# First mixer: rotary key columns first with their weights stationary, latents normed singly, query products between transposes

## The reference, cut to what matters

```python
def mla_mixer(h, cos, sin, w_in, g_qa, w_qb, g_kva, w_kvb, g_q, g_k, w_o):
    z = h @ w_in                                  # 2048 -> 512 + 512 + 64
    c_q, c_kv, k_rope = jnp.split(z, [512, 1024], axis=-1)
    q  = (rms_norm(c_q,  g_qa)  @ w_qb ).reshape(b, s, 16, 192)
    kv = (rms_norm(c_kv, g_kva) @ w_kvb).reshape(b, s, 16, 256)
    k_nope, v = jnp.split(kv, [128], axis=-1)
    k = concatenate([k_nope, k_rope for every head])
    q, k = rms_norm(q, g_q), rms_norm(k, g_k)     # over 192 columns of a head
    q, k = (each with its last 64 columns rotated by cos, sin)
    o = blocked_attention(q, k, v, 1 / sqrt(192), chunk_causal=True)
    return o.reshape(b, s, 2048) @ w_o
```

## Time and profile before

| | us |
|---|---|
| median of 3 runs | 3583.55 (3583.06 to 3585.41) |
| the profiled execution | 3579.43 |
| its span | 3577.5 |
| granted TensorE clock, mean | 0.917 of 2.4 GHz |

### The profile page before, as it was taken

How to read it: one execution, slowest core, us unless ns; L and a number is a source line. 1 busy time by engine, 2 the same in 40 slices (tenths; PEclk the granted TensorE clock), 3 DMA queues, 4 the chain that set the end, 5 groups by cost and what they waited for, 6 DMA issues and landing times.

```text
span 3577.5 us, 26686 instructions
## 1 busy us (share of the span) xinstructions
PE 2869.6 (80%) x7322; PEld 1347.5 (38%) x7322; DVE 2037.9 (57%) x3580; ACT 946.3 (26%) x2345; POOL 1422.9 (40%) x1065
## 2 busy tenths in 40 slices
PE   7888967777777888888878788998987877777776
PEld 6445743333332333333333333443433322222222
DVE  2334156666767554555554665455555466777765
ACT  3334322222222222323221222232322122222221
POOL 4002645565665322222432432322333255555553
PEclk8877989998998999999999899999999998888888
DMA  4212599999999999999999999999999999999998
GB/s 145 83 62 81 194 384 416 416 414 417 416 417 422 418 417 417 417 417 418 416 419 417 413 417 417 417 417 417 416 400 419 417 408 418 418 417 420 415 417 357
DMA packets 246468, 1345.34 MB, mean 376 GB/s; under 512 B 27200, under 2 KB 48192, under 8 KB 113984
## 3 DMA queue, kind: packets, MB, share of 16 engines
q0 software_dynamic: 147456, 1073.81, 72.5%
q1 hardware_dynamic: 98880, 269.99, 19.8%
HBM read 1341.62 MB, written 2.10 MB: 376 GB/s over the span
## 4 chain that ended last, share of the span: by engine, by line
DMA 64%; PE 20%; issue 11%; DVE 3%; POOL 1%; ACT 1%; SPq 1%; DVEq 0%; POOLq 0%; ACTq 0%
DMA room<-in_peer_v_dram,index 64%; PE psum L982 12%; PE psum L1033 3%; PE psum L745 1%; PE psum L746 1%; PE psum L747 1%; POOL room L673 1%; DVE room L1962 0%; DVE resid L1973 0%; POOL room L683 0%; DMA room<-in_peer_u_dram,index 0%; SPq L544 0%; POOL w_low L657 0%; SPq L514 0%; PE psum L948 0%
## 5 line engine op out<-in xcount | busy, mean ns | idle before, releaser
L982 PE MATMUL psum<-room,diag 128*128 128x512 f32 x3072 | 1636.2, 675 | 628.1 <-DMA room<-in_peer_v_dram,index 581.6
L1962 DVE CUSTOM_DVE_ANT_0 room<-room,normed 128x2048 f32<-128x2048 f32 x512 | 1172.9, 2291 | 664.4 <-DMA room<-in_peer_u_dram,index 660.0
L982 PEld LDWEIGHTS psum<-room,diag 128*128 128x128 f32 x3072 | 607.2, 210 | 1595.4 <-issue 1257.2
L683 POOL DMA_INDIRECT room<-in_peer_v_dram,index x512 | 748.5, 1462 | 1070.2 <-PE psum L982 1039.9
L673 POOL DMA_INDIRECT room<-in_peer_u_dram,index x512 | 558.3, 1090 | 757.9 <-DVE dots L1962 529.6
L1033 PE MATMUL psum<-wbuf,normedT 128*128 128x512 f32 x1536 | 695.1, 595 | 0.0
L1392 ACT ACTIVATE acts<-dots 128x1 f32<-128x1 f32 x512 | 103.6, 202 | 1832.2 <-DVE dots L1962 1831.8
L1973 DVE SCALAR_TENSOR_TENSOR resid<-room,acts,resid 128x512 f32<-128x512 f32 x512 | 384.4, 751 | 290.9 <-DMA room<-in_peer_v_dram,index 289.1
L1033 PEld LDWEIGHTS psum<-wbuf,normedT 128*128 128x128 f32 x1536 | 285.3, 191 | 330.7 <-issue 327.6
L657 POOL TENSOR_TENSOR w_low<-wbuf,w_high 128x2048 fp32r<-128x2048 f32 (+1 forms) x28 | 113.9, 4076 | 305.1 <-ACT w_high L1247 305.1
L1401 ACT ACTIVATE diag<-ident,acts 128x128 f32<-128x128 f32 x512 | 205.5, 401 | 48.3 <-ACT acts L1396 1.5
(11 more groups left out here) (197 smaller groups left out, 1742.8 us busy)
## 6 DMA issues: line engine op xcount, KB each, us to landing
wbuf<-in_fox_w_in_dram SPq DMA_DIRECT2D x128, 1024.0 KB
wbuf<-in_fox_w_o_dram SPq DMA_DIRECT2D x32, 1024.0 KB
wbuf<-in_peer_w_q_dram SPq DMA_DIRECT2D x32, 1024.0 KB
wbuf<-in_mla_w_o_dram SPq DMA_DIRECT2D x16, 1024.0 KB, 5.2
wbuf<-in_peer_w_q_dram SPq DMA_DIRECT2D x32, 512.0 KB, 8.9
wbuf<-in_mla_w_in_dram SPq DMA_DIRECT2D x8, 1024.0 KB, 8.2
wbuf<-in_mla_w_kvb_dram SPq DMA_DIRECT2D x32, 256.0 KB, 3.5
room<-in_peer_u_dram,index POOLq DMA_INDIRECT x512
```

The lines of the kernel that those rows point to most:

```text
L683: pool.indirect_dma_start(v_ring[:, r, :], None, v_table, bass.IndirectOffsetOnAxis(index[:, number % 2, s:s + 1], 0)).then_inc(v_full[r], 16)
L982: mm = pe.matmul(psum[:, q, :], diag[:, r, :], v_ring[:, r, q * TILE:(q + 1) * TILE], start=at == 0, stop=at == WINDOW - 1, skip_group_che ...
L1962: V.tensor_tensor_reduce(u_ring[:, r, :], u_ring[:, r, :], normed[:, b, :], 1.0, 0.0, ALU.mult, ALU.add, dots[:, r:r + 1]).then_inc(dot_do ...
```

## The change

1. The 64 rotary columns of `w_in` get a buffer of their own in `room`. SP loads them in one DMA ahead of the first tile; ACT and POOL split them behind the first quarter of that tile. PE multiplies them right behind the transposes of the normed tokens, with the weights (64 columns) stationary and the 256 tokens moving: 48 matmuls in place of 96. The result lies transposed and is turned back by two small transposes behind those of the sub-keys. DVE does the rotary keys first.
2. Each latent is normed by itself. The query latent's transposes stand inside the second tile, behind its sixth and seventh eighth.
3. The four query pieces of group g+1 stand one ahead of each of the four transposes of group g; the four key/value pieces behind the first four attention steps. ACT copies the query products ahead of the attention. Each weight buffer is given back by itself: that of keys/values behind T(q,1), that of queries behind the first attention step, the last one behind the last group's transposes.

The diff, cut to its core:

```diff
             w_in = rows_view(mla_w_in[0])
-            widths = (Q_RANK, KV_RANK, ROPE)
-            for t in range(3):
-                c0 = sum(widths[:t])
-                load_quarters(S_IN + t, 0, w_in, slice(c0, c0 + widths[t]), widths[t], free=t == 0)
+            sp.dma_start(rope_w, w_in[:, :, Q_RANK + KV_RANK:Q_RANK + KV_RANK + ROPE]).then_inc(rope_loaded, 16)
+            for t in range(2):
+                load_quarters(S_IN + t, 0, w_in, slice(t * Q_RANK, (t + 1) * Q_RANK), free=t == 0)
                 if t == 0:
                     small_operands()
...
-            for t, width in enumerate((Q_RANK, KV_RANK, ROPE)):
-                low_parts([S_IN + t], width)
+            pool.wait_ge(unit_high, 1)
+            pool.tensor_tensor(quarter(w_low, 0), values(0), quarter(w_high, 0), ALU.subtract).then_inc(unit_low, 1)
+            pool.wait_ge(rope_split, 1)
+            pool.tensor_tensor(rope_low[:, :, :], rope_w, rope_high[:, :, :], ALU.subtract).then_inc(rope_split2, 1)
+            low_parts([S_IN], 1)
+            low_parts([S_IN + 1])
...
+            def rope_keys():
+                pe.wait_ge(rope_split2, 1)
+                for k in range(KC):
+                    pe.matmul(dst, rope_high[:, k, :], x_high[:, k, :], start=k == 0, stop=False)
+                    pe.matmul(dst, rope_low[:, k, :], x_high[:, k, :], start=False, stop=False)
+                    last = pe.matmul(dst, rope_high[:, k, :], other[:, k, :], start=False, stop=k == KC - 1)
+                last.then_inc(rope_full, 1)
+            def rope_transposes():
+                pe.wait_ge(rope_out, 1)
+                for b in range(NB):
+                    last = transpose(psum[:, 6, T + b * ROPE:T + (b + 1) * ROPE],
+                                     raw_v[0:ROPE, 0, T + b * P:T + (b + 1) * P], ROPE)
+                last.then_inc(rope_turned, 1)
...
+                def turned(t, b):
+                    pe.wait_ge(lat_norm, 2 * t + b + 1)
+                    if t:
+                        pe.wait_ge(lat_done, b + 1)
+                    for c in range(RC):
+                        last = transpose(sbank(b)[:, c * P:(c + 1) * P], (qn, kn)[t][:, b, c * P:(c + 1) * P])
+                    last.then_inc(lat_full, 1)
+                split_gemm(S_IN, 0, Q_RANK, x_high, other)
+                split_gemm(S_IN + 1, 0, KV_RANK, x_high, other,
+                           steps=[lambda: None] * 5 + [lambda: turned(0, 0), lambda: turned(0, 1)])
+                for b in range(NB):
+                    turned(1, b)
+            def qk_transposes(at, g, kind, ahead):
                 src = (qn, kn)[kind]
                 for b in range(NB):
+                    if ahead:
+                        ahead.pop(0)()
                     at.qk_norm.done(pe, g, 2 * kind + b)
                     if kind == 0:
...
-                        if b == NB - 1 and t:
-                            for t2 in range(2):
-                                (wh, wn), (gh, gn) = mla.w(g, t2), mla.g(g, t2)
-                                pe.wait_ge(g_full[gh], 2 * gn + 2)
-                                pe.sem_inc(w_used[wh], 1)
...
+            def release(g, t):
+                (wh, wn), (gh, gn) = mla.w(g, t), mla.g(g, t)
+                pe.wait_ge(g_full[gh], 2 * gn + 2)
+                pe.sem_inc(w_used[wh], 1)
...
+                pe.wait_ge(lat_done, 2)
+                run(mla_products(0, 0))
                 pe.wait_ge(lat_done, 4)
-                run(mla_products(0))
+                kv = mla_products(0, 1)
+                run(kv[0:2])
+                release(0, 0)
+                run(kv[2:4])
                 with pe.Fori(0, mla.groups - 1) as g:
-                    for kind in range(2):
-                        qk_transposes(mla, g, kind)
-                    steps, pieces = attention(mla, g), mla_products(g + 1)
-                    for i in range(max(len(steps), len(pieces))):
-                        run(steps[i:i + 1])
-                        run(pieces[i:i + 1])
+                    ahead = mla_products(g + 1, 0)
+                    qk_transposes(mla, g, 0, ahead)
+                    release(g, 1)
+                    qk_transposes(mla, g, 1, ahead)
+                    steps, kv = attention(mla, g), mla_products(g + 1, 1)
+                    for i, step in enumerate(steps):
+                        step()
+                        if i == 0:
+                            release(g + 1, 0)
+                        run(kv[i:i + 1])
                 for kind in range(2):
-                    qk_transposes(mla, mla.groups - 1, kind)
+                    qk_transposes(mla, mla.groups - 1, kind, [])
+                release(mla.groups - 1, 1)
                 run(attention(mla, mla.groups - 1))
...
             norm_transposes(0)
+            rope_keys()
             sub_keys()
+            rope_transposes()
...
                     copy_transposed(p, b)
+                    if p == 0 and b == 0:
+                        act.wait_ge(rope_loaded, 16)
+                        nc.scalar.activation(rope_high[:, :, :], rope_w, ACT.Copy).then_inc(rope_split, 1)
...
+                high_parts(S_IN + 1, qs=range(3))
+                copied(0, raw_q)
+                high_parts(S_IN + 1, qs=range(3, 4))
+                root(0)
+                turned(0)
+                copied(1, raw_k)
+                root(1)
+                turned(1)
...
                 with act.Fori(0, mla.groups - 1) as g:
                     both_transposed(g)
-                    attention(mla, g, lambda step: step == COPY_Q_AT and copy_q(g + 1))
+                    copy_q(g + 1)
+                    attention(mla, g)
                     copy_kv(g + 1)
...
+            act.wait_ge(rope_full, 1)
+            nc.scalar.activation(raw_v[0:ROPE, 0, T:2 * T], psum[0:ROPE, 6, 0:T], ACT.Copy).then_inc(rope_out, 1)
             act.wait_ge(keys_full, 1)
             nc.scalar.activation(keysT[:, :, :], psum[:, 7, :].rearrange("p (m n) -> p m n", m=4),
                                  ACT.Copy).then_inc(keys_done, 1)
+            act.wait_ge(rope_turned, 1)
+            nc.scalar.activation(raw_v[:, :, 0:ROPE], psum[:, 6, T:T + 2 * ROPE].rearrange("p (b r) -> p b r", b=NB),
+                                 ACT.Copy).then_inc(rope_done, 1)
...
             def latent():
+                dve.wait_ge(rope_done, 1)
                 for b in range(NB):
...
                 chain.settle()
+                for t, (raw, g) in enumerate(((raw_q, g_qa), (raw_k, g_kva))):
+                    for b in range(NB):
+                        dve.wait_ge(evac[(G_IN + t) % 2], 2 * ((G_IN + t) // 2) + b + 3)
+                        last = sum_squares(raw[:, b, :], (qn, kn)[t][:, b, :], l_sum[:, 2 * t + b:2 * t + b + 1])
+                    last.then_inc(lat_ss, 1)
+                    dve.wait_ge(lat_root, t + 1)
+                    step(V.reciprocal(l_inv[:, 2 * t:2 * t + 2], l_root[:, 2 * t:2 * t + 2]))
+                    chain.settle()
+                    for b in range(NB):
+                        V.scalar_tensor_tensor(out=(qn, kn)[t][:, b, :], in0=raw[:, b, :],
+                                               scalar=l_inv[:, 2 * t + b:2 * t + b + 1], in1=g[:, :],
+                                               op0=ALU.mult, op1=ALU.mult).then_inc(lat_norm, 1)
```

More of the change, by code:

```diff
@@ L340, in hybrid_encoder @@
         unit_full = [sem(f"unit_full{q}") for q in range(4)]
+        rope_loaded, rope_split, rope_split2, rope_full, rope_out, rope_turned, rope_done = (
+            sem(n) for n in ("rope_loaded", "rope_split", "rope_split2", "rope_full", "rope_out", "rope_turned",
+                             "rope_done"))
         unit_high, unit_low, unit_used = sem("unit_high"), sem("unit_low"), sem("unit_used")
@@ L650, in _, with low_parts @@
             assert n[0] == N_CONST
-            def low_parts(tiles, width=TILE):
+            def low_parts(tiles, first=0):
                 for n in tiles:
-                    for q in range(4):
+                    for q in range(first, 4):
                         pool.wait_ge(unit_high, 4 * n + q + 1)
-                        pool.tensor_tensor(quarter(w_low, q, width), values(q, width),
-                                           quarter(w_high, q, width), ALU.subtract).then_inc(unit_low, 1)
+                        pool.tensor_tensor(quarter(w_low, q), values(q), quarter(w_high, q),
+                                           ALU.subtract).then_inc(unit_low, 1)
             def low_parts_looped(n0, tiles):
@@ L1852, in groups @@
                     else:
-                        attention(at, g, lambda s: s == COPY_Q_AT and head_norms(at, g + 1, 0, part=0))
+                        attention(at, g, lambda s: s == SQUARES_AT and head_norms(at, g + 1, 0, part=0))
                         head_norms(at, g + 1, 0, part=1)
```

65 lines of the change are left out of this document (20 added, 45 removed).

## The result

| | before | after |
|---|---|---|
| median, us | 3583.31 (3580.10 to 3585.41, 4 runs) | 3553.50 (3552.49 to 3555.44, 4 runs) |
| span of the profiled execution | 3577.5 | 3552.0 |
| granted TensorE clock, mean | 0.917 | 0.925 |

The ratio is 0.9918, with a 95% interval of 0.9905 to 0.9932: a gain of 24 to 34 us, 29.8 by the medians and 25.5 by the two traces. The prediction was 26.5.

What follows compares the result with a forecast made beforehand. Until the gathers start, everything hangs on PE in the first mixer. Start gains 9.8, groups 17.7, output weights cost 1.0: 26.5 us, so 3557.0 against the median of 3583.55; range 3546 to 3574.

Steps and rivals of the forecast that it cites:

- first products: Group 0's first products on PE, behind the key/value latent's chain and transposes, were to start at 83.8.
- attention + tail: Within a group: attention 15.0 us; tail, from last output transpose to next logits, 10.6 + 0.8 + 1.0 us.
- output weights late: At group 7, the last weight buffer comes free only with T(k,1); output weights 0.5 to 1.6 late, cost 1.0.
- The rotary load: Ahead of the first tile: 0.5 MB in 256-byte pieces makes the first weight quarter 2.3 us later.
- The start: Everything up to group 0's logits, with the third tile gone: logits at 105.5 against 115.31, a gain of 9.8 us.
- the query weights: Ahead of group 0's products: SP may load them from 79.0 on, and they need 4 to 5 us.
- The group: Loop over groups: 27.4 us each, the last 25.6; seven intervals 190.0 against 207.7, a gain of 17.7 us.
- Rival (a): The clock never falls in a tail: 26.4 us a group, 6 us more gain, 3551; chance 14%.
- unbroken work: In each tail, 6 us of unbroken pieces and transposes behind the gap will raise the clock before the attention.
- forecast of 3 to 7 us: Sign to look for: a cold stretch of 3 to 7 us in each tail and none in the attention.
- Rival (c): Key/value weights late by 1.5 us in each group: minus 9, 3566; 17% together with a tail between forecast and old rhythm.
- Rival (b): Old rhythm stays, clock low some 13 us in each group: gain of 7.5 less 1.0, 3577; chance 11%.

Runs made afterwards that it cites:

- Experiment 9: Changed start and old group loop with idle-time filling products, plus rotary load behind the first weight quarter and two more fillings: 3541.19 us, ratio 0.9881.
- experiment 3: Kernel of before with 3, 5 and 7 dummy products filling PE's idle time in each tail: 3551.45 us in one run.
- experiment 4: Changed kernel with nine dummy products between the first query piece and T(q,0): 3556.97 us in one run.
- experiment 6: Changed kernel with the query pieces ahead of the four transposes as 2, 0, 1, 1 and not 1, 1, 1, 1: 3557.55 us in one run.
- experiment 10: Kernel of before with 2, 2 and 3 dummy products in PE's idle time in each tail: 3562.89 us in one run.
- experiment 2: Kernel of before with the changed group loop and the old start: 3561.76 us, ratio 0.9942.
- experiment 7: Changed kernel with the last weight buffer released ahead of the last group's transposes, not behind them: 3555.89 us in one run.
- experiment 8: Changed kernel with the key/value weight buffer given back behind T(k,1), not T(q,1): 3580.39 us in one run.
- experiment 1: Changed start with the group loop of the kernel before: 3570.92 us, ratio 0.9973.

## Why the prediction was right

Step by step, the prediction's number and then the trace of the changed kernel:

| step | predicted | measured |
|---|---|---|
| first quarter later by | 2.3 | 2.42 (15.91 against 13.49) |
| first rotary product | 25.6 | 25.57 |
| first tile starts | 34.5 | 34.76 |
| second tile ends | 79.0 | 79.6 (SP's next load at 79.93) |
| first products | 83.8 | 85.36 |
| logits of group 0 | 105.5 | 107.00 |
| attention + tail | 15.0 + 12.4 | 15.3 + 12.1 |
| interval | 27.4, last 25.6 | 27.35, last 25.66 |
| output weights late | 1.0 | 1.35 |
| sum | 26.5 | 25.5 in the traces, 29.8 in the medians |

**The rotary load** landed as the row of 128 KB in 0.57 us had it, not after the 1.7 us that I had estimated from the Trainium skill, DMA: Bandwidth & Descriptors, section Why small descriptors are slow: 0.5 MB in 2.42 us is some 217 GB/s. Experiment 9 confirms the other side: with the load second, the conversion starts at 13.74.

**The start was mis-sized by 1.5 us** (9.8 predicted, 8.3 measured). The term is the one on the query weights: "need about as long, 4 to 5 us". They needed 5.4 us from SP's issue at 79.93 to PE's first product, and I had counted the 4 to 5 us from 79.0, the second tile's end, which came at 79.6. PE waited 1.36 us for them; without that wait the products would have begun at 84.0, where I had 83.8. Experiment 9 shows it by making the latent's side faster: the wait for the weights then grows, and the 5.4 us stay.

**The group was right in sum, and in what it said of the clock.** There is a gap between the first piece and T(q,0) (2.38 us, 3.1 predicted), the clock is low there or behind it, and it is up again before the attention; the cost is 0.8 us, 1.0 predicted. That the clock was the reason for the groups' gain, and not the number of instructions, is shown by experiments 3, 4, 6 and 10. Rival (a), a clock that never falls, was put at 26.4 us a group: it is 26.5 to 26.8 in the groups of experiments 4 and 6 where the clock held. The prediction gave 4.5 of the old 30.7 us to the clock; it is 5.0. The other 0.5 lay in the tail, whose 10.6 us it took for its length at the full clock; with the clock held it is 10.2 (157.86 to 168.01 in experiment 3, filling and all). So the new order is in itself 0.8 us longer than the old, where the prediction had 0.2 (26.4 against 26.2).

**One reason was not shown.** The prediction had the clock rise before the attention because 6 us of unbroken work follow the gap. It did rise, but unbroken work is not enough to say when. In the kernel before, PE worked without a gap through the first 10 us of the attention, at the low clock all the time:

```profile
169.50:179.60 10.10, 10.10 (x21) 0.50 0.00 0
```

In the profiles of the changed kernel and of experiments 2, 4, 6 and 7 the low stretch was 3.4 or 6.8 us in every steady group that had one, and none reached the attention; so the forecast of 3 to 7 us held. Why it is short there stays open, and as far as the forecast rested on the unbroken work it had luck.

**Rival (c)**, late key/value weights, did not come, but only by the margin: experiment 8 moved their release by one step and had the interval at 30.7. I had priced a late load at its own length (1.5 us late, 1.5 us a group); there it cost twice its wait, since the clock fell behind it. Rival (b)'s gain of 7.5 us is 7.7 by its own terms, which leaves its 3577.

**The output weights**: experiment 7 gives the 1.35 us back in full, so the step's mechanism is shown.

**The gap between 25.5 and 29.8.** The interval of the ratio (24 to 34 us) holds both. The prediction worked from before's profiled execution and put its forecast 4.1 us higher for the median, since that execution lay so far below it; the changed kernel's profiled execution was 3553.9, only 0.4 above its median. So the 3557.0 was 3.5 us high mostly by which execution of before was profiled, not by a step of the sum; that the sum met the traces within 1 us and the medians within 3.3 is as close as these runs can tell. The stretch behind group 7's logits, from 3253 to 3261 us in the kernels here, is where such differences arise; what makes it vary stays open.

## What to carry to other kernels

Where TensorE waits on a chain of other engines again and again, read the granted clock beside the waits before moving any work: here 5 of 30.7 us per group were the clock, and idle-time products, without any reordering, gained 28 us in the one run made of them. Work moved into such a gap also cut what the low clock cost (5.0 to 0.8 us), but the moved order was itself 0.8 us longer. When a buffer's release moves, look for the first reader behind the reload and for what is queued on its engine: a wait of 1.65 us cost 3.4.

## What the runs showed of the hardware that was not expected

The low stretch has several lengths: 13.6 us in each steady group of before and of experiment 1, 6.8 in experiments 2 and 7, 3.4 in the changed kernel and in experiments 4, 6 and 10; experiment 8 has one of 6.8 and one of 3.4 in a group. The instructions don't settle it: experiment 7 has the loop of the changed kernel. Nor does work without gaps: PE was busy all of 10.1 us at the low clock in the attention of before (169.5 to 179.6), and in experiment 10 the clock rose within 4 us of such work (144 to 148). What sets the length stays open.

At the same instructions the clock may fall in one group and not in the next (experiment 6: two groups of 26.6 to 26.8 us and four of 27.3 to 27.4; experiment 10: three and four), so a loop near that edge has two times.

The filling products cost their neighbours little. Seven plain float32 products of 128 columns took 1.73 us. T(q,0) stands 5.1 us behind the last output transpose with them (157.59 to 162.68) and 4.5 without (189.32 to 193.81), but the whole tail is 10.2 us with them and 10.6 without, where its end ran at the low clock. And the groups of experiment 10 in which the clock held take 25.6 to 25.7 us (the first apart), as in experiment 3 with twice the filling.
